# The end of the second scan and the entry of attention, put in another order, in a two-layer hybrid trunk step

## The reference

```python
# C: gla_scan, forward and (flipped) backward, q, k, v in chunks
cum = jnp.cumsum(lf, axis=2)
...
chunk_state = jnp.einsum('bcjhk,bcjhv->bchkv', kc * jnp.exp(last - cum), vc)
...
o_inter = jnp.einsum('bcihk,bchkv->bcihv', qc * jnp.exp(cum), s_in)
# hgrn_mixer
o = rms_norm(o_f + flip_t(o_b), p['hgrn_norm']...) * jax.nn.silu(g...)
# A: queries and the shared key are rotated, keys are [own 64 | rotated 32]
q_a = jnp.concatenate([q_a[..., :NOPE_A], axial_rope(q_a[..., NOPE_A:])], axis=-1)
k = jnp.concatenate([kv[..., :NOPE_A], jnp.broadcast_to(kr, ...)], axis=-1)
o_a = dense_attention(q_a, k_a, v_a, None)
```

## Time and profile before

| what | value |
|---|---|
| median of 3 runs | 3118.11 us (3109.12 to 3118.77) |
| the profiled execution, its own time | 3118.77 us |
| its span, first to last instruction | 3117.0 us |
| TensorE busy, its weight load | 2940.1 us (94%), 2603.6 us (84%) |
| VectorE, ScalarE busy | 1290.1 us (41%), 905.9 us (29%) |
| mean granted TensorE clock | 0.972 of full speed |

### The profile page before, as it was taken

One profiled execution on the slowest core, in us unless ns is written; L12 is line 12 of the kernel. 1 busy time (PEld: TensorE's weight loads), 2 busy tenths in 40 slices (PEclk: granted clock), 3 DMA queues, 4 the chain that ended last, 5 costly groups with the idle time before them and its releaser, 6 DMA issues.

```text
span 3117.0 us, 46405 instructions
## 1 busy us (share of the span) xinstructions
PE 2940.1 (94%) x20109; PEld 2603.6 (84%) x20109; DVE 1290.1 (41%) x1813; ACT 905.9 (29%) x1262; POOL 35.2 (1%) x32
## 2 busy tenths in 40 slices
PE   6999999998889899999979999999998998999997
PEld 5999998776645599999979999977775556999996
DVE  3223236436554622322542332364284636223236
ACT  3221223323443322122252222233243514222222
POOL 0000000100000000000000000001000000000000
PEclk8999999999989999999989999999998999999998
DMA  9223234104120321322532222421142013223211
GB/s 305 68 60 87 76 114 129 54 14 122 55 89 14 95 82 55 87 81 78 159 109 77 66 82 77 140 80 54 28 135 86 30 28 95 78 59 87 81 56 53
DMA packets 359017, 259.03 MB, mean 83 GB/s; under 512 B 27152, under 2 KB 310100, under 8 KB 358740
## 3 DMA queue, kind: packets, MB, share of 16 engines
q1 hardware_dynamic: 358868, 256.85, 27.3%
HBM read 253.25 MB, written 3.57 MB: 82 GB/s over the span
## 4 chain that ended last, share of the span: by engine, by line
PE 89%; DVE 7%; ACT 2%; DMA 1%; issue 1%; SPq 1%; ACTq 0%; DVEq 0%
PE banks L743 57%; PE banks L653 17%; PE banks L603 1%; PE banks L1193 1%; PE banks L1029 1%; PE banks L857 1%; PE banks L1216 1%; DVE x_res L1836 1%; PE banks L1230 1%; ACT arena L1279 1%; PE banks L1186 1%; DVE w_split L1716 1%; PE banks L923 1%; PE banks L908 1%; PE banks L1134 1%
## 5 line engine op out<-in xcount | busy, mean ns | idle before, releaser
L743 PE MATMUL banks<-h_hi,w_split 128*128 128x320 f32 x5376 | 1185.1, 309 | 2.1 <-DVE mod L1665 2.1
L743 PEld LDWEIGHTS banks<-h_hi,w_split 128*128 128x128 f32 x5376 | 899.3, 188 | 2.9 <-issue 2.9
L743 PE MATMUL banks<-h_lo,w_split 128*128 128x320 f32 x2688 | 830.6, 309 | 0.0
L743 PE MATMUL banks<-hid_hi,w_split 128*128 128x320 f32 x2816 | 624.0, 309 | 0.1
L1279 ACT ACTIVATE arena<-banks 128x640 f32<-128x640 f32 (+8 forms) x336 | 171.7, 537 | 1235.4 <-PE banks L743 886.6
L1716 DVE TENSOR_TENSOR w_split<-w_slots,w_split 128x2048 fp32r<-128x2048 f32 x152 | 348.4, 2292 | 421.0 <-ACT w_split L1279 421.0
L743 PEld LDWEIGHTS banks<-h_lo,w_split 128*128 128x128 f32 x2688 | 504.6, 188 | 0.0
L743 PEld LDWEIGHTS banks<-hid_hi,w_split 128*128 128x128 f32 x2816 | 471.7, 188 | 1.7 <-issue 1.2
L743 PE MATMUL banks<-hid_lo,w_split 128*128 128x320 f32 x1408 | 435.1, 309 | 0.0
L1279 ACT ACTIVATE w_split<-w_slots 128x2048 fp32r<-128x2048 f32 x152 | 290.1, 1908 | 403.5 <-PE banks L743 397.0
L1780 DVE TENSOR_TENSOR arena<-arena,banks 128x640 f32<-128x640 f32 x88 | 72.3, 821 | 752.2 <-ACT arena L1279 752.2
(11 more groups left out here) (261 smaller groups left out, 2394.2 us busy)
## 6 DMA issues: line engine op xcount, KB each, us to landing
w_slots<-in_ffn_w_gu SPq DMA_DIRECT2D x176, 512.0 KB, 5.1
arena<-in_w_mod SPq DMA_DIRECT2D x14, 2048.0 KB, 12.5
w_slots<-in_ffn_w_down SPq DMA_DIRECT2D x64, 384.0 KB, 3.6
w_slots<-in_ffn_w_down SPq DMA_DIRECT2D x64, 320.0 KB, 4.3
h_mod<-in_w_mod SPq DMA_DIRECT2D x8, 2048.0 KB, 8.0
w_slots<-in_w_mod SPq DMA_DIRECT2D x8, 2048.0 KB, 9.1
mixed<-in_w_mod SPq DMA_DIRECT2D x6, 2048.0 KB, 9.2
w_slots<-in_w_in SPq DMA_DIRECT2D x6, 2048.0 KB, 7.9
```

The source lines that it names most:

```text
L743: ins = mm(banks[:, b0 + hf, 0:HALF], w[:, k, :], x[:, k, t], start=w is wlo and k == 0, stop=w is whi and x is hi and k == kt - 1, skip_g ...
```

## The change

Nothing is computed otherwise; instructions move and waits are split. On VectorE the products of `KF` with `SE` and `KB` with `PB` go into the last round of levels, ahead of the modulation add, and the copies into `SIN` ahead of `merge(7)`; ScalarE makes the exponentials in the order `SE`, `PB`, `PF`, `SI`. TensorE's turning of the keys waits for two products in place of four, and for the merges of banks 0 and 1, then 2 and 3, as it comes to them. ScalarE's squares into `SQA` get a new wait for the fourth product. The output norm's first part moves from after rotation 0 to after rotation 1, and its last product is split in two that follow rotations 2 and 3. Key head 3 goes behind the values and `rotate(7)`, on TensorE and ScalarE, with the job order changed to match. The copies of the rotated key go between the evacuations of query heads 1, 2 and 3. `attn_in_act` is gone; the first four scores wait for one query's rotation each, and `new_ready` is waited for after score 1.

```diff
@@ -132,7 +132,7 @@
...
     number = {name: (s, n) for s, names in enumerate(SLOT_FILLS) for n, name in enumerate(names)}
-    jobs = ["msq", "mskv", "y1", "q0", "ms1"] + [f"q{h}" for h in range(1, 4)] + [f"k{h}" for h in range(4)] + ["va"]
+    jobs = ["msq", "mskv", "y1", "q0", "ms1"] + [f"q{h}" for h in range(1, 4)] + ["k0", "k1", "k2", "va", "k3"]
     jobs += [f"o{m}" for m in range(KT_M)]
@@ -1049,15 +1049,17 @@
...
-                pe.wait_ge(s["fin_prod"], o["fin_prod"] + 4)
-                pe.wait_ge(s["att_used"], o["att_used"] + 3 * (LEVELS + 1))
+                pe.wait_ge(s["fin_prod"], o["fin_prod"] + 2)
                 for c in range(NCH):
+                    if c in (0, 2):
+                        pe.wait_ge(s["att_used"], o["att_used"] + 3 * LEVELS + c // 2 + 1)
                     if c >= 4:
...
                 pe.wait_ge(s["k_copied"], o["k_copied"] + NCH)
+                pe.wait_ge(s["att_used"], o["att_used"] + 3 * (LEVELS + 1))
@@ -1092,6 +1094,7 @@
...
                 pe.wait_ge(s["sin_ready"], o["sin_ready"] + 1)
+                pe.wait_ge(s["fin_prod"], o["fin_prod"] + 4)
                 b0 = slot(job["y1"])
@@ -1146,14 +1149,17 @@
...
                 pe.wait_ge(s["cache_ready"], o["cache_ready"] + 1)
-                for h in range(4):
+
+                def keys(h):
                     j = job[f"k{h}"]
...
                     mm(banks[0:NOPE, slot(j) + 2, 0:256], wk, CKN[:, LAT:EXT], start=True, stop=True).then_inc(s["done"], 1)
-                    if h < 3:
-                        rotate(4 + h)
+
+                for h in range(3):
+                    keys(h)
+                    rotate(4 + h)
                 j = job["va"]
@@ -1162,11 +1168,13 @@
...
                 rotate(7)
-
-                pe.wait_ge(s["attn_in_act"], o["attn_in_act"] + 1)
+                keys(3)
+
+                pe.wait_ge(s["roped"], o["roped"] + 4)
                 nc.tensor.transpose(banks[:, 7, 0:P], CKN[:, LAT:TOK], ident)
...
                 nc.tensor.transpose(banks[:, 7, 2 * P:2 * P + QK_A], KR[0:QK_A, LAT:TOK], ident[0:QK_A, 0:QK_A]).then_inc(s["new_turned"], 1)
+
                 def score(u):
@@ -1174,6 +1182,8 @@
...
                     if un["kind"] == "A":
+                        if u < 4:
+                            pe.wait_ge(s["roped"], o["roped"] + 5 + u)
                         q = QA[0:QK_A, un["h"], un["q"]:un["q"] + P]
@@ -1195,9 +1205,7 @@
...
-                pe.wait_ge(s["roped"], o["roped"] + 8)
                 pe.wait_ge(s["kcopied"], o["kcopied"] + 2)
-                pe.wait_ge(s["new_ready"], o["new_ready"] + 1)
                 pe.wait_ge(s["pool_load"], o["pool_load"] + 16)
@@ -1219,6 +1227,7 @@
...
                 score(1)
+                pe.wait_ge(s["new_ready"], o["new_ready"] + 1)
                 for u in range(len(units)):
@@ -1558,13 +1567,14 @@
...
                 link(f(DEC[:, 1], ends(SI, 0), ACT.Exp))
-                for ap in (PF, SI, SE, PB):
+                for ap in (SE, PB, PF, SI):
                     f(ap, ap, ACT.Exp).then_inc(s["fin_exp"], 1)
...
                     f(KTOK[:, c], banks[:, c % 4, :].rearrange("p (d n) -> p d n", d=4)).then_inc(s["k_copied"], 1)
+                act.wait_ge(s["fin_prod"], o["fin_prod"] + 4)
                 f(SQA[:, 0], CQ[0], ACT.Square).then_inc(s["aq_sq"], 1)
@@ -1594,20 +1604,22 @@
...
                     evacuate(f"q{h}", both(f"q{h}", QA[0:QK_A, h], QK_A))
-                for h in range(4):
+                    if h < 3:
+                        act.wait_ge(s["roped"], o["roped"] + 1)
+                        f(KA[NOPE:QK_A, 2 * h - 2:2 * h, :], bc(KR[NOPE:QK_A, :].unsqueeze(1), [ROPE, 2, EXT])).then_inc(s["kcopied"], 1)
+
+                def keys_out(h):
                     b0 = slot(job[f"k{h}"])
                     evacuate(f"k{h}", [(banks[0:NOPE, b0, :], KA[0:NOPE, h, 0:LAT]), (banks[0:NOPE, b0 + 2, 0:256], KA[0:NOPE, h, LAT:EXT])])
+
+                for h in range(3):
+                    keys_out(h)
                 b0 = slot(job["va"])
...
                 evacuate("va", [(pair(banks[:, b0 + i, :]), VA[:, 2 * i:2 * i + 2, :]) for i in range(3)])
-                for p in range(2):
-                    act.wait_ge(freed[p], o["freed"][p] + len([j for j in range(job["va"] + 1) if j % 2 == p]))
-                act.sem_inc(s["attn_in_act"], 1)
+                keys_out(3)
                 act.wait_ge(s["new_turned"], o["new_turned"] + 1)
                 finish(f(NEWROWS[:, 0:2 * P + QK_A], banks[:, 7, 0:2 * P + QK_A]), "new_ready", 1)
-                act.wait_ge(s["roped"], o["roped"] + 1)
-                for i in range(2):
-                    f(KA[NOPE:QK_A, 2 * i:2 * i + 2, :], bc(KR[NOPE:QK_A, :].unsqueeze(1), [ROPE, 2, EXT])).then_inc(s["kcopied"], 1)
@@ -2056,23 +2068,25 @@
...
                     v.tensor_tensor(k2, k2, halves(KB, m)[1], ALU.mult).then_inc(s["prods"], 1)
+                    if lev == LEVELS:
+                        dve.wait_ge(s["prods"], o["prods"] + 3 * LEVELS)
+                        for i, (x, y) in enumerate(((KF, SE), (KB, PB))):
+                            dve.wait_ge(s["fin_exp"], o["fin_exp"] + i + 1)
+                            v.tensor_tensor(x, x, y, ALU.mult).then_inc(s["fin_prod"], 1)
                     if lev - 1 in RING_AT:
                         mod_add(l, RING_AT[lev - 1], 7, 2 * P)
-                merge(LEVELS)
-                dve.wait_ge(s["fin_exp"], o["fin_exp"] + 4)
-                for x, y in ((PF, Q), (SI, Q)):
-                    v.tensor_tensor(x, x, y, ALU.mult).then_inc(s["fin_prod"], 1)
-                for x, y in ((KF, SE), (KB, PB)):
-                    v.tensor_tensor(x, x, y, ALU.mult).then_inc(s["fin_prod"], 1)
-                if LEVELS in RING_AT:
-                    mod_add(l, RING_AT[LEVELS], 7, 2 * P)
-
                 dve.wait_ge(s["sin_zero"], o["sin_zero"] + 1)
...
                         link(v.tensor_copy(SIN[rows, 3 * d, 2 * d:2 * d + 2, rows], src[rows, 2 * d:2 * d + 2, :]))
+                merge(LEVELS)
+                dve.wait_ge(s["fin_exp"], o["fin_exp"] + 4)
+                for x, y in ((PF, Q), (SI, Q)):
+                    v.tensor_tensor(x, x, y, ALU.mult).then_inc(s["fin_prod"], 1)
+                if LEVELS in RING_AT:
+                    mod_add(l, RING_AT[LEVELS], 7, 2 * P)
                 for t in range(4):
@@ -2110,13 +2124,15 @@
...
                     finish(v.tensor_tensor(ap, ap, ROT[0:rows], ALU.add), "roped", n + 1)
-                    if n == 0:
+                    if n == 1:
                         dve.wait_ge(s["y_rstd"], o["y_rstd"] + 1)
...
                                                         op0=ALU.mult, op1=ALU.mult))
-                        link(v.tensor_tensor(MIX[:, 4:6], Y, MIX[:, 4:6], ALU.mult))
-                        dve.sem_inc(s["mixed_ready"], 1)
+                    elif n in (2, 3):
+                        link(v.tensor_tensor(MIX[:, n + 2], Y[:, n - 2], MIX[:, n + 2], ALU.mult))
+                        if n == 3:
+                            dve.sem_inc(s["mixed_ready"], 1)
...
                     un = units[u]
```

More of the change, by code:

```diff
@@ L355, in trunk_kernel @@
                  "y_ready ysq y_rstd excl_zero f_raw f_ready mixed_ready "
-                 "aq_sq aq_rstd aq_norm akv_norm cache_turned cache_ready rot_done rot_used roped kcopied attn_in_act "
+                 "aq_sq aq_rstd aq_norm akv_norm cache_turned cache_ready rot_done rot_used roped kcopied "
                  "new_turned new_ready scored maxed expd p_turned p_copied pv_done scaled on_used "
```

2 lines of the change are left out of this document (1 added, 1 removed).

## The result

The changed kernel takes **3076.42 us** (median of 4 runs, 3073.89 to 3078.15). The kernel before, run beside it, takes 3116.94 us (3109.12 to 3118.77), so the ratio is 0.987, with a 95% interval of 0.9858 to 0.9882. That is 40.5 us less, where 46.2 were forecast. One later run of the changed kernel took 4593.97 us at a mean granted clock of 0.592 and enters no figure.

A forecast was written before the change was run, and what follows sets the result against it. TensorE was taken as the bound (89% of the chain), its waits paid in the gap and again in a lower clock behind. 8.3 + 12.3 + 2.5 = 23.1 us a layer, 46.2 for two, gave 3072 us, range 3060 to 3084.

The forecast's parts named there:

- Part 1: Scan's end: early key products and split waits let the chunk states start sooner; 8.3 us a layer.
- two thin covers: Scan's end: early key products fit into VectorE's idle 3.11 and 1.02 us; without cover the merge comes 2.9 us later.
- Part 2: Rotations and attention's entry: moved norm and later key head 3 bring the first score forward; 12.3 us a layer.
- costed at nothing: Rotated-key copies, 2.85 us, hidden between ScalarE's query heads; if that cover failed, TensorE would wait 1.4 us.
- Part 3: Attention's first units at the upper clock: 2.5 us a layer, between bounds of nothing and 4.0.
- Sum: Scan's end, rotations and entry, first units: 8.3 + 12.3 + 2.5 = 23.1 us a layer, 46.2 for two.
- does nothing but come earlier: Argument that the gain reaches the end: 89% of the chain lies on TensorE, only 1% on DMA.
- its 0.3 and 1.4 us: Gaps forecast between the transposes at the scan's end; only longer ones were said to end in clock 0.50.
- Rival 1: Clock falls at the scan's end all the same, costing 2.1 to 6.5 us a layer: 3076 to 3085; chance 0.25.
- Rival 2: VectorE becomes the bound, by uncovered early products or norm parts holding up rotations: 3076 to 3082; chance 0.08.
- Rivals 3 and 4: 3: gain does not reach the end, 3118, chance 0.03; 4: clock stays down from scan's end, 3186, chance 0.02.

The follow-up runs named there:

- e4: Changed kernel with five of the six value products ahead of rotation 7 made twice in each layer; 3074.81 us, ratio 0.9873.
- e9: Changed kernel with unit 36's score product made four times over, in front of the 0.87 us gap in attention; 3071.37 us, ratio 0.9855.
- e5: Changed kernel with the four short units of the fifth tile second in each attention branch, not last; 3068.91 us, ratio 0.9843.
- e8: Changed kernel run once more, nothing altered; 3074.77, 3076.44 and 3077.91 us.
- e7: Changed kernel with one wait for all the last merges ahead of the turned keys, in place of the split one; 3074.20 us, ratio 0.9863.
- e10: Kernel before the change with only e5's unit order; 3132.98 us, ratio 1.0044, twelve runs in three groups.
- e12: Changed kernel with e5's unit order plus e4's doubled value products; 3078.77 us, ratio 0.9876.
- e13: The same kernel as e5, run again in five rounds; 3069.20 us, ratio 0.9848.

## Why the prediction was right

The time, 3076.42 us, lies in the range, and at the three places the forecast's mechanism is what the trace shows; the figure of 3072 was 4.5 us too low.

- **Part 1, 8.3 us.** Chunk states were to start 3.9 us behind level 7's products, and start 3.64 behind them. The squares were to cost 0.2 us and cost 0.4. Together 12.40 - 3.64 - 0.41 = 8.35 us. The two thin covers held: the merge waits 0.20 us for TensorE, so it is still TensorE that comes last.
- **Part 2, 12.3 us.** Chunk states to first score went from 69.12 to 57.71 us, and with the 0.41 that Part 1 already carries this is 11.8. What was costed at nothing cost next to nothing: the copies of the rotated key made TensorE wait nowhere, and of the norm's pieces one held back one rotation a little: it starts 0.69 us behind the product ahead of it, its neighbours 0.52, so 0.17 us were lost.
- **Part 3, 2.5 us.** It measured 2.91 (11.84 - 8.93), in the upper half of its bounds of 0 and 4.0.
- **Sum, 23.1 us a layer.** It measured 23.08. That it is so close is luck: Part 2 was 0.5 us too high, Part 3 0.4 too low.
- **The step that failed** is that this sum was set equal to the gain in time: TensorE behind the entry "does nothing but come earlier". It came earlier, but with another clock: 4.4 us a layer given back in the profiled execution. The prediction had a term for the clock at each wait that goes, and none for places with short gaps that stay. Its sentence that only longer gaps than its 0.3 and 1.4 us were seen to end in 0.50 does not hold of the kernel before: there the clock fell at 986.1 us, in layer 1 and alike in layer 2, behind gaps of at most 0.96. e4 shows that this was the clock and not a wait, and e9 and e5 agree; e8 shows an execution in which most of this loss is missing.
- **Luck in the time.** The profile after gives back 8.8 us by the clock, but 5.5 are won elsewhere that are not the change's, as e8 shows. So the two profiled executions lie 42.8 us apart, 3.4 short of the 46.2. The other 2.3 up to the 5.7 by which the medians fall short is where these executions lie: 1.83 us over their median before, 0.48 under it after.
- **Rival 1** names a time, 3076 to 3085, that holds the measured one, but its mechanism did not occur: in 808.6 to 812.0 us TensorE did nothing but 20 transposes, with gaps of 0.21 and 0.79 us beside them, at a granted clock of 1.00. e7 shows that it stays up over gaps of 1.99 and 0.90 us there, too. By the rule of the Trainium skill (TensorE: Matmul & The Clock Gate, Part 4: PE-mode transpose) that transposes do not count as work for the gate in the way that products do, these 3.4 us, and 5.3 in e7, are idle time to it; the traces disagree, since the clock stayed at 1.00 in both and, in the kernel before, rose from its lower level over nothing but the 20 transposes.
- **Rival 2** did not occur, but for that 0.17 us: the merge still waits for TensorE, and no rotation's product stands in the list of waits. **Rivals 3 and 4** did not: the gain reached the end but for the clock, and the chunk states to the first score ran at 1.00.

Open: what made the start and the work behind the two projections 2.58, 1.84 and 1.05 us quicker in one execution of the changed kernel and not in e8's was not tried; nor was what decides whether a gap of 0.9 or 1.3 us loses the clock.

## What to carry to other kernels

A wait in front of TensorE can be paid twice, in the gap and in the clock behind it (behind e7's 1.99 us the clock stayed at 1.00), and both can be read off and added up; three such places gave 23.08 us a layer where 23.1 were forecast. But every gap that stays in the program may trip the clock anew when the work ahead of it is shifted, so a sum of this kind needs a few us of room on either side, and a variant should be judged by the spread of many runs and not by one profile. Filling or moving a gap can be worth more than the work it costs, but in the middle of attention's small products a fall was dear (e10): look at what follows before choosing where the gap goes.

## What the runs showed of the hardware

- The same instructions with the same gap lose the clock in one execution or layer and keep it in another (0.88 us in e10's two layers; 0.87 us after, and 0.88 at the same place in e8; 1.29 us in e12 and e13).
- How long the lower level lasts differs much: 37.5 us in attention's small products, with TensorE busy for 37.50 of them (e10), against 3.4 us where the projection's products followed at once (e4). What follows is not all: at one place, with the same products behind it, it was 3.4 us in one layer and 10.2 in the other (e12).
- Added work can cost less than nothing (e9, three products of 1.16 - 0.48 = 0.68 us added in a layer, and 5 us won in all) and much more than itself (e12, 2.16 us added in a layer, and 9.6 lost in all).
